# A diagonal recurrence beside latent attention: turning tables made one stage earlier, and four products summed on TensorE

## The chip, the cores and the metric

The kernel runs on one core of a Trainium2 chip. The metric is the device time in microseconds of one launch, the median of several runs. The engines are TensorE (PE in the profile; its weight loads PEld), VectorE (DVE), ScalarE (ACT), GpSimd (POOL) and SyncE (SP), which issues the weight DMAs. They run their own instruction streams and meet at semaphores.

## The reference, cut to what matters

Eight blocks follow each other on 512 positions of 1024 channels: four of a first network, then two layers of a second, each a mixer and a feed-forward block. The change concerns the mixer of the second layer (stage "o") and the feed-forward block ahead of it (stage "f0"). Stage o projects the input once, runs a diagonal state-space recurrence on 256 of the channels and a latent attention of 6 heads on the others, and multiplies both by the output weights:

```
proj = t @ w_in
y_c = s5_ssm(proj[..., :256], ...)            # recurrence
y_d = mla_attention(c_q, c_kv, k_r, ...)      # attention
out = concatenate([y_c, y_d]) @ w_out

# s5_ssm: complex state of 16 groups x 64, mag and angle per state from a_re, a_im, log_dt
x[s] = (mag * exp(i * angle)) * x[s-1] + bu[s]
y = x_re @ c_re - x_im @ c_im + d_skip * u
z = gelu(y);  y_c = z * sigmoid(z @ w_glu + b_glu)
```

## The kernel before, in words

Everything stays in SBUF; activations are kept transposed (128 channels by 512 positions a tile). Each fp32 product is made of three fp32r matmuls (`product`, L286 to L299): high weights by high activations, high by low, low by high. Weights come in units of 128 by 1024 through two raw buffers and four slots. SyncE loads a unit when VectorE has split the one two before it, ScalarE makes its high part (`split_high`, L276), VectorE its low part (`split_low`, L283). The splits are called three units ahead (`AHEAD`).

A feed-forward stage works in three groups of 8, 8 and 6 tiles of gate and up products with a SiLU between them and an output product behind each group; `tail_*` and `head_*` carry one stage into the next by halves of the positions. While a stage's norm is still being summed, its first four units are multiplied unnormed and scaled later by the reciprocal root (`late_keep`, L424).

**Stage o** follows a list written out by hand, `o_events` (L2086), which all engines walk through: "head" (units 0 to 3), "bu" (input products of a state tile), "u" (units 4 and 5), "state n" (VectorE's recurrence up to instruction n), "sum" and "norm" (the norms of the latent tiles), "kn", "v", "uq" (keys, values, queries), "cy" (output products of a state tile), then 27 "step"s: in step n the scores of block n, the softmax of it on VectorE and ScalarE, the transposes of block n-2 and the values of block n-3. Every step takes up to four state instructions with it, until all are done.

**The recurrence** has eight state tiles of 128 states. Turning the state by its angle makes the complex recurrence two real ones, each a scan (`tensor_tensor_scan`). Per tile VectorE issues 14 instructions, all counted on the semaphore `o_ssm` (L2554 to L2592): 0 to 5 turn the products of `bu` (in PSUM banks 2 and 3) back by the table of cosines and sines, 6 and 7 are the scans, 8 to 13 turn the result forward: four multiplications, a subtraction and an addition give the two parts x_re and x_im in `full`. TensorE multiplies these by `o_c` (L2222), two fp32 matmuls of 32 output rows a tile; each stands as two records in the trace.

**The tables** are made on GpSimd inside stage o (`o_gpsimd`, L2688). By doubling, it makes cosines and sines of 32 fine and 16 coarse positions for all eight tiles; for each tile a wide product of both gives the 512 cosines and sines, six operations of 128 by 512 (L2693, L2737). The buffer `o_e` holds two tiles; tile j waits until tile j-2's 14 instructions are done. The small tables wait for stage e's output, and the fine one is copied when stage o's norm is summed.

**The head of stage o**: ScalarE (L2334 to L2346) runs for m = 0 to 2 a weight split and then copies the product out, and for m = 3 it first keeps the norm scale; VectorE (L2602) does three splits, waits for the scale and scales the two tiles of u, which "bu" needs. VectorE also scales c's coefficients after state instruction 8 (`prepare_c`), and turns one rotary tile per "uq" (`rope`), with `o_w` (that is `ssq`) as scratch, as in the state instructions.

Of the kernel before, what the change touches and what calls it, by code (L numbers as in the profile page):

```python
# [31 lines left out]
P = 128  # L32
# [125 lines left out]
def build(nc, stream, x_in, params_in, const_in, tables_in, ssm_in, x_out):  # L158
# [10 lines left out]
    with ctx:  # L169
# [86 lines left out]
        o_c_done, o_small_done = sem("o_c_done"), sem("o_small_done")  # L256
        o_e_done, o_lin, o_squared, o_sums, o_roots = sem("o_e_done"), sem("o_lin"), sem("o_squared"), sem("o_sums"), sem("o_roots")
        o_rstds, o_normed, o_n_high, o_n_low = sem("o_rstds"), sem("o_normed"), sem("o_n_high"), sem("o_n_low")
        o_rot, o_turned, o_cosed, o_roped = sem("o_rot"), sem("o_turned"), sem("o_cosed"), sem("o_roped")
        o_bu, o_ssm, o_cy, o_taken, o_gelu = sem("o_bu"), sem("o_ssm"), sem("o_cy"), sem("o_taken"), sem("o_gelu")  # L260
# [1824 lines left out]
        O_SSM, O_BANKS, O_PER_STEP = 14, 5, 4  # L2085
        O_STEPS = NBLK * MLA_HEADS + 3  # L2086

        def o_events():

            out = [("head", 0), ("bu", 0), ("state", 8), ("u", 4), ("bu", 1), ("state", 14), ("sum", 0),  # L2090
                   ("cy", 0), ("state", 22), ("u", 5), ("bu", 2), ("state", 28), ("cy", 1), ("sum", 1), ("norm", 0),
                   ("state", 36), ("kn", 0), ("v", 0), ("bu", 3), ("uq", 0), ("state", 42), ("uq", 1), ("cy", 2)]
# [40 lines left out]
        o_tmp = work[:, 1536:2048]  # L2133
        o_ea = work[:, 2048:2304].rearrange("p (c j n) -> p c j n", c=2, j=SSM_TILES)
        o_eb = sq[:].rearrange("p (c j n) -> p c j n", c=2, j=SSM_TILES)
# [11 lines left out]
        O_SOFT = 3  # L2147
        O_EVENTS = o_events()
# [28 lines left out]
        def o_tensor(pe, t, first, o, y_base, r, last=False):  # L2177
# [17 lines left out]
            for event, n in O_EVENTS:  # L2195
# [17 lines left out]
                if event == "cy":  # L2213
# [7 lines left out]
                    for c in range(2):  # L2221
                        mm = nc.tensor.matmul(out, o_c[:, c, m], full[:, c], start=c == 0, stop=c == 1,  # L2222
                                              tile_position=(0, 32 * (m % 4)))
# [101 lines left out]
        def o_scalar(act, first, o, y_base, r, last=False):  # L2325
# [7 lines left out]
            for event, n in O_EVENTS:  # L2333
                if event == "head":  # L2334
                    norm_root(act, R_PRE["o"])
                    for m in range(4):
                        u = Unit(first + m)
                        if m == 3:
                            act.wait_ge(table_loaded, 16 * (TABLED.index("o") + 1))
                            late_keep(act, "o", 7, o_r)  # L2340
                        else:
                            split_high(act, u + 1 + AHEAD)
# [3 lines left out]
                        copy((o_us[:, 0], o_us[:, 1], o_lat[:, 0], o_lat[:, 1])[m], m, (units_done, u.count(1)))  # L2346
                if event == "u":
# [59 lines left out]
                if event == "gelu":  # L2407
                    for m in range(2):
                        act.wait_ge(o_taken, m + 1)
                        nc.scalar.activation(o_us[:, m], o_us[:, m], ACT.Gelu_apprx_tanh).then_inc(o_gelu, 1)  # L2410
                    for m in range(2):
                        act.wait_ge(o_gelu, m + 1)
# [100 lines left out]
        def o_vector(dve, first, o, y_base, r, last=False):  # L2513
# [4 lines left out]
            def rope(n, bank, tile):  # L2518

                dve.wait_ge(o_rot, n + 1)  # L2520
                nc.vector.tensor_tensor(o_w[:], bank, table[:, T:2 * T], ALU.mult).then_inc(o_turned, 1)
# [577 lines left out]
```

## Time and profile before

| what | value |
|---|---|
| median of 3 runs (lowest, highest) | 3076.29 us (3073.81, 3078.74) |
| profiled execution, its span | 3078.95 us, 3077.1 us |
| PE busy, share of the span | 2950.9 us, 96% |
| DVE busy | 1753.1 us, 57% |
| ACT busy | 1061.6 us, 35% |
| POOL busy | 200.3 us, 7% |
| chain that ended last | PE 81%, DVE 10%, ACT 3%, issue 3%, POOL 2% |
| mean granted TensorE clock | 0.976 |

Stage f0 runs from about 2035 to 2440 us and stage o's own work from about 2430 to 2720 us of the span. In the tables below a line number is the line of the kernel; "idle" is the time for which the engine did nothing before an instruction, with what ended it. Overlapping instructions of one engine can start before the one ahead has ended, so the distance of two starts is the better price of one.

### The profile page before, as it was taken

To read this page: it belongs to the slowest core of one execution; us is meant where nothing else is said; L and a number is where in the kernel's file an instruction comes from. 1 tells how busy PE (TensorE), PEld (TensorE's weight loads), DVE (VectorE), ACT (ScalarE), POOL (GpSimd) and SP (SyncE) were. 2 spreads that over 40 slices of the span, in tenths; PEclk is the share of its full clock that TensorE was granted. 3 is DMA by queue.
4 is the path that set the end of the run, shared out by engine and by line. 5 is a ranking of instruction groups with operands and counts; after the bars stand their busy time and mean duration, and the time that the engine had idled before them with its cause. 6 is when DMAs were issued, how large, how long until landed. Compare 5 with 4: busy or idle time off the path is not lost.

```text
span 3077.1 us, 38456 instructions
## 1 busy us (share of the span) xinstructions
PE 2950.9 (96%) x14106; PEld 2411.0 (78%) x14106; DVE 1753.1 (57%) x2644; ACT 1061.6 (35%) x1596; POOL 200.3 (7%) x203
## 2 busy tenths in 40 slices
PE   8999999999999999999999999899999778899998
PEld 6888888888888778878888866588888744788887
DVE  5554536764676576653545586564444588464445
ACT  4332323442344332233322424442223423442222
POOL 1000000000000100000000100020000533110001
PEclk9999999999999999999999999899999888999999
DMA  4232232212221223333232321023333210123332
GB/s 144 96 96 94 85 106 73 60 58 83 75 60 57 83 82 98 97 94 102 83 101 90 103 70 41 16 93 108 94 102 96 69 41 7 55 89 96 95 96 89
DMA packets 70399, 252.12 MB, mean 82 GB/s; under 512 B 7808, under 2 KB 9856, under 8 KB 69632
## 3 DMA queue, kind: packets, MB, share of 16 engines
q1 hardware_dynamic: 68112, 241.89, 25.7%
q10 hardware_dynamic: 2160, 8.49, 0.8%
q8 instruction: 86, 1.41, 0.2%
q14 instruction: 41, 0.34, 0.0%
HBM read 248.25 MB, written 2.10 MB: 81 GB/s over the span
## 4 chain that ended last, share of the span: by engine, by line
PE 81%; DVE 10%; ACT 3%; issue 3%; POOL 2%; DMA 0%; DVEq 0%; ACTq 0%; POOLq 0%
PE ps L296 17%; PE ps L298 17%; PE ps L297 17%; PE ps L567 2%; PE ps L568 2%; PE ps L569 2%; DVE w_low L283 2%; ACT w_high L276 2%; PE ps L778 1%; PE ps L779 1%; PE ps L780 1%; PE ps L1788 1%; PE ps L852 1%; PE ps L590 1%; PE ps L838 1%
## 5 line engine op out<-in xcount | busy, mean ns | idle before, releaser
L283 DVE TENSOR_TENSOR w_low<-raw,w_high 128x1024 fp32r<-128x1024 f32 x456 | 562.2, 1238 | 421.0 <-ACT w_high L276 413.7
L296 PE MATMUL ps<-h_high,w_high 128*128 128x512 f32 x1872 | 738.7, 395 | 5.7 <-DVE arena L1463 3.0
L298 PE MATMUL ps<-h_high,w_low 128*128 128x512 f32 x1872 | 730.7, 390 | 0.0
L297 PE MATMUL ps<-h_low,w_high 128*128 128x512 f32 x1872 | 730.5, 390 | 0.0
L276 ACT ACTIVATE w_high<-raw 128x1024 fp32r<-128x1024 f32 x456 | 477.8, 1051 | 454.8 <-PE ps L298 214.2
L296 PEld LDWEIGHTS ps<-h_high,w_high 128*128 128x128 f32 x1872 | 352.9, 189 | 80.7 <-issue 4.6
L298 PEld LDWEIGHTS ps<-h_high,w_low 128*128 128x128 f32 x1872 | 352.4, 188 | 74.2
L297 PEld LDWEIGHTS ps<-h_low,w_high 128*128 128x128 f32 x1872 | 353.0, 189 | 70.1
L296 PE MATMUL ps<-y_high,w_high 128*128 128x512 f32 x640 | 250.3, 391 | 0.6 <-DVE y_low L1923 0.2
L297 PE MATMUL ps<-y_low,w_high 128*128 128x512 f32 x640 | 249.1, 389 | 0.0
L298 PE MATMUL ps<-y_high,w_low 128*128 128x512 f32 x640 | 249.0, 389 | 0.0
L324 POOL TENSOR_TENSOR root<-root,ssq 128x512 f32<-128x512 f32 x24 | 33.0, 1373 | 1691.8 <-ACT ssq L312 1690.4
L296 PEld LDWEIGHTS ps<-y_high,w_high 128*128 128x128 f32 x640 | 120.1, 188 | 27.8 <-DVE y_low L685 2.0
L298 PEld LDWEIGHTS ps<-y_high,w_low 128*128 128x128 f32 x640 | 120.1, 188 | 25.3
L297 PEld LDWEIGHTS ps<-y_low,w_high 128*128 128x128 f32 x640 | 120.2, 188 | 24.7
L567 PE MATMUL ps<-w_high,h_high 128*128 128x512 f32 x256 | 102.1, 399 | 11.5 <-DVE w_low L283 11.5
L568 PE MATMUL ps<-w_low,h_high 128*128 128x512 f32 x256 | 101.4, 396 | 0.0
L569 PE MATMUL ps<-w_high,h_low 128*128 128x512 f32 x256 | 101.1, 395 | 0.0
L1549 ACT ACTIVATE y_high<-full 128x512 f32 (+1 forms) x44 | 27.8, 632 | 192.6 <-DVE full L1579 192.6
L778 PE MATMUL ps<-w_high,h_high 128*128 128x512 f32 x192 | 76.7, 400 | 3.2 <-DVE x L519 2.1
L779 PE MATMUL ps<-w_low,h_high 128*128 128x512 f32 x192 | 76.0, 396 | 0.0
L780 PE MATMUL ps<-w_high,h_low 128*128 128x512 f32 x192 | 75.8, 395 | 0.0
(403 smaller groups left out, 4573.8 us busy)
## 6 DMA issues: line engine op xcount, KB each, us to landing
raw<-stream SPq DMA_DIRECT2D x456, 512.0 KB, 3.6
table<-tables_in ACTq DMA_DIRECT2D x5, 1088.0 KB, 6.6
x<-x_in ACTq DMA_DIRECT2D x8, 256.0 KB, 8.5
x_out<-x SPq DMA_DIRECT2D x16, 128.0 KB, 1.7
const<-const_in SPq DMA_DIRECT2D x1, 673.0 KB, 8.0
work<-ssm_in ACTq DMA_DIRECT2D x1, 512.0 KB, 3.7
params<-params_in ACTq DMA_DIRECT2D x1, 287.0 KB, 6.8
```

Source lines behind the costliest of these rows:

```text
L276: nc.scalar.activation(w_high[:, u.slot], raw[:, u.raw], ACT.Copy).then_inc(weights_high, 1)
L283: nc.vector.tensor_tensor(w_low[:, u.slot], raw[:, u.raw], w_high[:, u.slot].bitcast(F32), ALU.subtract).then_inc(weights_low, 1)
L296: nc.tensor.matmul(bank, wh, high[:, k], start=k == 0, stop=False)
L297: nc.tensor.matmul(bank, wh, low[:, k], start=False, stop=False)
L298: mm = nc.tensor.matmul(bank, wl, high[:, k], start=False, stop=k == tiles - 1)
L324: nc.gpsimd.tensor_tensor(root[:], root[:], (sq, ssq)[m % 2][:], ALU.add).then_inc(norm_gathered, 1)
L567: nc.tensor.matmul(bank, hh, wh, start=k == 0, stop=False)
L568: nc.tensor.matmul(bank, hh, wl, start=False, stop=False)
L569: mm = nc.tensor.matmul(bank, hl, wh, start=False, stop=k == KD - 1)
L778: nc.tensor.matmul(bank, hh, wh, start=k == 0, stop=False)
L779: nc.tensor.matmul(bank, hh, wl, start=False, stop=False)
L780: mm = nc.tensor.matmul(bank, hl, wh, start=False, stop=k == KD - 1)
```

## The change

The tables are made in a function `o_tables` that GpSimd runs at the start of stage f0, once stage e's residual is added. Tiles 0 and 1 are written to `o_e`, where they stay. Tiles 2 to 7 go through a ring of five buffers in a part of the arena that the feed-forward stage doesn't use, and are stored to a DRAM tensor, 512 KB each. In stage o, GpSimd fetches tile j from there into `o_e` when tile j-2's instructions are done. VectorE waits for the fetch instead of for the computation.

A tile takes 12 instructions on VectorE in place of 14. The four products of the forward turn go to four buffers (`full`, `sq`, `o_w`), one with its sign changed, and cy adds them on TensorE: four matmuls with the same `o_c` in place of two. VectorE's scratch is now `o_t` in `work`. The event list has the counts of 12. In the head, the keeping of the norm scale goes ahead of the third weight split on ScalarE, and the scaling of u ahead of it on VectorE; the split of that unit follows behind the head's copies. The semaphore `o_gelu` is merged into `o_z_high`.

```diff
@@ -2082,14 +2083,14 @@
-O_SSM, O_BANKS, O_PER_STEP = 14, 5, 4
+O_SSM, O_BANKS, O_PER_STEP = 12, 5, 4
...
-    out = [("head", 0), ("bu", 0), ("state", 8), ("u", 4), ("bu", 1), ("state", 14), ("sum", 0),
-           ("cy", 0), ("state", 22), ("u", 5), ("bu", 2), ("state", 28), ("cy", 1), ("sum", 1), ("norm", 0),
-           ("state", 36), ("kn", 0), ("v", 0), ("bu", 3), ("uq", 0), ("state", 42), ("uq", 1), ("cy", 2)]
+    out = [("head", 0), ("bu", 0), ("state", 8), ("u", 4), ("bu", 1), ("state", 12), ("sum", 0),
+           ("cy", 0), ("state", 20), ("u", 5), ("bu", 2), ("state", 24), ("cy", 1), ("sum", 1), ("norm", 0),
+           ("state", 32), ("kn", 0), ("v", 0), ("bu", 3), ("uq", 0), ("state", 36), ("uq", 1), ("cy", 2)]
@@ -2130,9 +2131,12 @@
 o_c = work[:, 1024:1536].rearrange("p (c j h) -> p c j h", c=2, j=SSM_TILES)
-o_tmp = work[:, 1536:2048]
+o_tmp = work[:, 0:512]
+o_t = work[:, 1536:2048]
 o_ea = work[:, 2048:2304].rearrange("p (c j n) -> p c j n", c=2, j=SSM_TILES)
-o_eb = sq[:].rearrange("p (c j n) -> p c j n", c=2, j=SSM_TILES)
+o_eb = work[:, 1536:2048].rearrange("p (c j n) -> p c j n", c=2, j=SSM_TILES)
+o_made = view(5120, 5, 2, T)
+o_kept = nc.dram_tensor("o_turns", (SSM_TILES, P, 2 * T), F32, kind="Internal").ap()
@@ -2145,6 +2149,7 @@
 O_SOFT = 3
+O_STORED = 16 * (SSM_TILES - 2)
@@ -2218,8 +2223,8 @@
             out = ps[32 * (m % 4):32 * (m % 4) + 32, 4]
-            for c in range(2):
-                mm = nc.tensor.matmul(out, o_c[:, c, m], full[:, c], start=c == 0, stop=c == 1,
+            for c, product_of in enumerate((full[:, 0], full[:, 1], sq[:], o_w[:])):
+                mm = nc.tensor.matmul(out, o_c[:, c // 2, m], product_of, start=c == 0, stop=c == 3,
@@ -2332,18 +2337,20 @@
         if event == "head":
+            act.wait_ge(o_e_moved, O_STORED)
...
                 u = Unit(first + m)
-                if m == 3:
+                if m < 2:
+                    split_high(act, u + 1 + AHEAD)
+                if m == 2:
...
                     late_keep(act, "o", 7, o_r)
-                else:
-                    split_high(act, u + 1 + AHEAD)
...
                 copy((o_us[:, 0], o_us[:, 1], o_lat[:, 0], o_lat[:, 1])[m], m, (units_done, u.count(1)))
+            split_high(act, Unit(first + 3 + AHEAD))
@@ -2407,9 +2414,9 @@
                 act.wait_ge(o_taken, m + 1)
-                nc.scalar.activation(o_us[:, m], o_us[:, m], ACT.Gelu_apprx_tanh).then_inc(o_gelu, 1)
+                nc.scalar.activation(o_us[:, m], o_us[:, m], ACT.Gelu_apprx_tanh).then_inc(o_z_high, 1)
             for m in range(2):
-                act.wait_ge(o_gelu, m + 1)
+                act.wait_ge(o_z_high, m + 1)
@@ -2518,11 +2525,11 @@
         dve.wait_ge(o_rot, n + 1)
-        nc.vector.tensor_tensor(o_w[:], bank, table[:, T:2 * T], ALU.mult).then_inc(o_turned, 1)
+        nc.vector.tensor_tensor(o_t, bank, table[:, T:2 * T], ALU.mult).then_inc(o_turned, 1)
...
         dve.wait_ge(o_cosed, n + 1)
-        nc.vector.tensor_tensor(tile, tile, o_w[:], ALU.add).then_inc(o_roped, 1)
+        nc.vector.tensor_tensor(tile, tile, o_t, ALU.add).then_inc(o_roped, 1)
@@ -2554,22 +2561,25 @@
             cos, sin = o_e[:, j % 2, 0], o_e[:, j % 2, 1]
-            b_re, b_im, x_re, x_im = ps[:, 2], ps[:, 3], full[:, 0], full[:, 1]
+            b_re, b_im = ps[:, 2], ps[:, 3]
...
                 dve.wait_ge(o_bu, j + 1)
-                dve.wait_ge(o_e_done, 2 * j + 2)
+                if j < 2:
+                    dve.wait_ge(o_e_done, 2 * SSM_TILES)
+                else:
+                    dve.wait_ge(o_e_moved, O_STORED + 16 * (j - 1))
...
             if n == 1:
-                op(j, o_w[:], sin, b_im, ALU.mult, 0)
+                op(j, o_t, sin, b_im, ALU.mult, 0)
             if n == 2:
-                op(j, o_a[:], o_a[:], o_w[:], ALU.add, 2)
+                op(j, o_a[:], o_a[:], o_t, ALU.add, 2)
...
             if n == 4:
-                op(j, o_w[:], sin, b_re, ALU.mult, 3)
+                op(j, o_t, sin, b_re, ALU.mult, 3)
             if n == 5:
-                op(j, o_s[:], o_s[:], o_w[:], ALU.subtract, 5)
+                op(j, o_s[:], o_s[:], o_t, ALU.subtract, 5)
@@ -2578,17 +2588,15 @@
                     dve.wait_ge(o_cy, j)
-                op(j, x_re, cos, o_a[:], ALU.mult, 7)
+                op(j, full[:, 0], cos, o_a[:], ALU.mult, 7)
             if n == 9:
-                op(j, o_w[:], sin, o_s[:], ALU.mult, 8)
+                dve.wait_ge(o_ssm, O_SSM * j + 8)
+                nc.vector.scalar_tensor_tensor(out=full[:, 1], in0=sin, scalar=-1.0, in1=o_s[:], op0=ALU.mult,
+                                               op1=ALU.mult).then_inc(o_ssm, 1)
             if n == 10:
-                op(j, x_re, x_re, o_w[:], ALU.subtract, 10)
+                op(j, sq[:], sin, o_a[:], ALU.mult, 8)
             if n == 11:
-                op(j, x_im, cos, o_s[:], ALU.mult, 8)
-            if n == 12:
-                op(j, o_w[:], sin, o_a[:], ALU.mult, 11)
-            if n == 13:
-                op(j, x_im, x_im, o_w[:], ALU.add, 13)
+                op(j, o_w[:], cos, o_s[:], ALU.mult, 8)
@@ -2600,12 +2608,13 @@
             norm_rstd(dve, R_PRE["o"])
-            for m in range(3):
+            for m in range(2):
...
                 nc.vector.tensor_tensor(o_us[:, m], o_us[:, m], o_r, ALU.mult).then_inc(o_us_scaled, 1)
+            split_low(dve, Unit(first + 3 + AHEAD))
@@ -2685,7 +2694,7 @@
-def o_gpsimd(pool):
+def o_tables(pool):
@@ -2695,10 +2704,8 @@
     pool.wait_ge(o_prepared, 1)
-    if "e" in names:
-        pool.wait_ge(out_free, 8 * (O_NO["e"] + 1) + 2)
-    early = o_e[:, 1].rearrange("p c (j n) -> p c j n", j=SSM_TILES)[:, :, :, 0:EB]
-    for tab, size, power in ((early, EB, 0), (o_ea, EA, 5)):
+    pool.wait_ge(post_added, 2 * KD * (P_NO["e"] + 1))
+    for tab, size, power in ((o_eb, EB, 0), (o_ea, EA, 5)):
@@ -2718,24 +2725,30 @@
             n, power = 2 * n, power + 1
-    pool.wait_ge(norm_summed, SUMMED[R_PRE["o"]] + 2)
-    nc.gpsimd.tensor_copy(o_eb, early).then_inc(o_small_done, 1)
-    pool.wait_ge(o_small_done, done[0] + 1)
-    done[0] += 1
...
         b_cos_, b_sin_ = (o_eb[:, c, j].unsqueeze(1).to_broadcast(shape) for c in range(2))
-        e_cos, e_sin = (o_e[:, j % 2, c].rearrange("p (a b) -> p a b", a=EA) for c in range(2))
+        target = o_e[:, j] if j < 2 else o_made[:, (j - 2) % 5]
+        e_cos, e_sin = (target[:, c].rearrange("p (a b) -> p a b", a=EA) for c in range(2))
         tmp = o_tmp.rearrange("p (a b) -> p a b", a=EA)
-        if j >= 2:
-            pool.wait_ge(o_ssm, O_SSM * (j - 1))
+        if j == 7:
+            pool.wait_ge(o_e_moved, 16 * 5)
...
             pool.wait_ge(o_e_done, 2 * j + (1 if op == ALU.subtract else 2))
+        if j >= 2:
+            pool.dma_start(o_kept[j], target.rearrange("p c t -> p (c t)")).then_inc(o_e_moved, 16)
+
+def o_gpsimd(pool):
+
+    for j in range(2, SSM_TILES):
+        pool.wait_ge(o_e_moved, O_STORED + 16 * (j - 2))
+        pool.wait_ge(o_ssm, O_SSM * (j - 1))
+        pool.dma_start(o_e[:, j % 2].rearrange("p c t -> p (c t)"), o_kept[j]).then_inc(o_e_moved, 16)
@@ -2852,6 +2865,8 @@
             e_gpsimd(pool)
+        if name == "f0":
+            o_tables(pool)
```

## Rows read from the trace of the kernel before

**Rows 1.** Stage f0 by stretch: length, PE, PEld, DVE, ACT, POOL busy, PEclk, DMA, GB/s.

```profile
2200.00:2300.00 100.00, 100.00 (x443) 82.79 (x442) 44.02 (x49) 25.77 (x30) 0.00 (x0) 1.00 0.32 97
```

**Rows 2.** Waits in stage o: total, times, longest.

```profile
PE ps L2222 <- DVE full L2550: 14.8, 5, 7.7
...
PE ps L2210 <- DVE arena L2608: 6.3, 1, 6.3
...
DVE root L2550 <- POOL arena L2737: 14.6, 1, 14.6
```

**Rows 3.** VectorE in order of time, stage o: start, length, instruction.

```profile
2443.39 1.23 DVE L283 TENSOR_TENSOR w_low<-raw,w_high 128x1024 fp32r<-128x1024 f32 x1 [3.46 <-ACT w_high L276]
2444.84 1.30 DVE L2608 TENSOR_TENSOR arena<-arena,table 128x512 f32<-128x512 f32 x2 [0.23 <-ACT table L424]
2460.77 0.69 DVE L2550 TENSOR_TENSOR root<-arena,ps 128x512 f32<-128x512 f32 x1 [14.63 <-POOL arena L2737]
...
2470.42 0.42 DVE L2535 TENSOR_TENSOR ssq<-work,small 128x256 f32<-128x256 f32 x1
...
2472.81 1.22 DVE L283 TENSOR_TENSOR w_low<-raw,w_high 128x1024 fp32r<-128x1024 f32 x1
...
2498.46 0.16 DVE L2624 SCALAR_TENSOR_TENSOR table<-ps,norm_col 128x4 f32<-128x4 f32 x1 [5.63 <-PE ps L2230]
...
2506.81 0.69 DVE L2550 TENSOR_TENSOR root<-arena,ps 128x512 f32<-128x512 f32 x1
...
2513.03 2.36 DVE L283 TENSOR_TENSOR w_low<-raw,w_high 128x1024 fp32r<-128x1024 f32 x2
...
2525.78 0.69 DVE L2550 TENSOR_TENSOR full<-arena,root 128x512 f32<-128x512 f32 x1
...
2529.76 1.23 DVE L283 TENSOR_TENSOR w_low<-raw,w_high 128x1024 fp32r<-128x1024 f32 x1
```

**Rows 4.** Busy time by stretch, stage o.

```profile
2439.90:2446.20 6.30, 0.00 (x1) 0.00 (x1) 2.55 (x4) 3.90 (x7) 5.38 (x14) 0.92 0.57 172
2446.20:2455.20 9.00, 9.00 (x17) 5.29 (x18) 0.00 (x0) 0.53 (x1) 7.21 (x24) 0.50 0.14 52
...
2535.30:2561.80 26.50, 24.28 (x72) 11.80 (x73) 24.49 (x50) 10.05 (x26) 11.07 (x9) 0.81 0.00 0
2574.60:2620.20 45.60, 39.98 (x142) 19.94 (x141) 41.99 (x89) 17.26 (x46) 7.38 (x6) 0.85 0.00 1
2620.20:2631.40 11.20, 11.20 (x51) 6.20 (x52) 4.95 (x20) 6.96 (x18) 0.00 (x0) 1.00 0.00 0
```

**Rows 5.** TensorE in order of time, stage o.

```profile
2477.95 3.62 PE L2222 MATMUL ps<-full,work 128*32 128x512 f32 x4 [7.66 <-DVE full L2550]
...
2487.70 1.98 PE L2210 MATMUL ps<-arena,work 32*128 32x512 f32 x4
...
2496.41 1.95 PE L2230 MATMUL ps<-const,arena 128*128 128x1 f32 x16
...
2530.57 1.90 PE L2222 MATMUL ps<-full,work 128*32 128x512 f32 x4
```

**Rows 6.** ScalarE in order of time, head of stage o.

```profile
2438.57 0.58 ACT L2329 ACTIVATE arena<-ps 128x512 f32<-128x512 f32 x1
2442.30 1.06 ACT L276 ACTIVATE w_high<-raw 128x1024 fp32r<-128x1024 f32 x1 [3.14 <-DMA raw<-stream]
...
2444.21 0.60 ACT L424 ACTIVATE table<-ps 128x512 f32<-128x512 f32 x1
```

**Rows 7.** GpSimd's groups from 1990 to 2720 us: busy, mean ns, idle before.

```profile
L2737 POOL TENSOR_TENSOR arena<-arena,work 128x512 f32<-128x512 f32 x16 | 24.4, 1525 | 1.3
...
L2693 POOL TENSOR_TENSOR work<-work,sq 128x512 f32<-128x512 f32 x16 | 18.1, 1128 | 1.3
```

**Rows 8.** TensorE's waits at the start of stage f0.

```profile
PE ps L296 <- DVE arena L1571: 0.5, 1, 0.5
```

**Rows 9.** DMA issues of the page: count, size, time to landing.

```profile
raw<-stream SPq DMA_DIRECT2D x456, 512.0 KB, 3.6
```

More of the change, by code:

```diff
@@ L256, in build @@
         o_c_done, o_small_done = sem("o_c_done"), sem("o_small_done")
+        o_e_moved = sem("o_e_moved")
         o_e_done, o_lin, o_squared, o_sums, o_roots = sem("o_e_done"), sem("o_lin"), sem("o_squared"), sem("o_sums"), sem("o_roots")
@@ L259, in build @@
         o_rot, o_turned, o_cosed, o_roped = sem("o_rot"), sem("o_turned"), sem("o_cosed"), sem("o_roped")
-        o_bu, o_ssm, o_cy, o_taken, o_gelu = sem("o_bu"), sem("o_ssm"), sem("o_cy"), sem("o_taken"), sem("o_gelu")
+        o_bu, o_ssm, o_cy, o_taken = sem("o_bu"), sem("o_ssm"), sem("o_cy"), sem("o_taken")
         o_z_high, o_z_low, o_sig, o_gated, o_small = sem("o_z_high"), sem("o_z_low"), sem("o_sig"), sem("o_gated"), sem("o_small")
@@ L2649, in o_vector @@
                 if event == "uq":
-                    assert at % O_SSM in (0, 8)
+                    assert at % O_SSM not in (2, 5)
                     rope(n + 1, ps[:, o_turn_bank(n)], o_q[:, n % 2, 2])
@@ L2675, in o_vector @@
                     for m in range(2):
-                        dve.wait_ge(o_z_high, m + 1)
+                        dve.wait_ge(o_z_high, m + 3)
                         nc.vector.tensor_tensor(h_low[:, 3 + m], o_us[:, m], h_high[:, 3 + m].bitcast(F32),
```

## The prediction

> **What bounds the kernel now.** The page comes first: TensorE is busy 96% of the span, so time can only be won where it is not. The busy table by stretch and TensorE's waits then lead to stage o. In the feed-forward stage before it TensorE has no gap in 100 us [rows 1]; in stage o it waits for VectorE: 14.8 us for the state products ahead of the cy matmuls, 6.3 us for the scaled u [rows 2]. VectorE's own waits show what is behind it: it stands 14.6 us for GpSimd's first turning table [rows 2]. The order in time says what surrounds that: VectorE is ready at 2444.84 + 1.30 = 2446.1, its first state product starts at 2460.77, and the argument of the second norm is taken at 2498.46 [rows 3]. From there to the first scores the stage is a mixed chain over all engines; in the softmax steps that follow, TensorE and VectorE are both nearly full, at a granted clock of 0.81 and 0.85 [rows 4].
>
> Two properties matter. While GpSimd builds tables, the first eight state instructions of a tile take 2470.42 - 2460.77 = 9.65 us; with GpSimd silent they take 2513.03 - 2506.81 = 6.2 [rows 3]. The 3.4 us between lie on the two additions and two scans: 0.86 each. And TensorE's clock falls behind idle time: after the 6.3 us gap it is 0.50 for 9 us [rows 4]; four cy records took 3.62 us cold and 1.90 warm [rows 5].
>
> **Head.** ScalarE keeps the norm scale only behind a weight split that waits 3.14 us for its DMA, at 2444.21 [rows 6]. The change puts it ahead of that split. ScalarE is free at 2438.57 + 0.58 = 2439.15 [rows 6]; it keeps the scale until 2439.75, and two squares and two copies, each some 0.48 behind the last, end at 2441.7. VectorE scales u meanwhile (1.30 us, [rows 3]), from 2439.9 to 2441.3. So bu of tile 0 starts at 2441.75 instead of 2446.2, after 1.9 us of idle, in which I expect the clock to stay (0.92 is its mean over all of the 6.3 us gap, [rows 4]). It takes 1.98 warm [rows 5], until 2443.7. Behind the scaling VectorE now has the split of unit 6, whose weights come when they came before: it ends at 2443.39 + 1.2 = 2444.6 [rows 3], and there the state products start, 16.1 us earlier than at 2460.77.
>
> **To the second norm sum, walked forward.** VectorE: eight instructions 6.2 us (2450.85); the coefficients of c, 2472.81 - 2470.42 = 2.4 [rows 3], and a split of 1.2 (2454.45); then the second half of the tile. That was six instructions in 2529.76 - 2525.78 = 4.0 us [rows 3]; it becomes four independent ones at 0.6, 2.45 us. The new scalar_tensor_tensor is priced like the others; at 1 us it would cost 0.4 a tile. Tile 0 is ready at 2456.9. TensorE, warm: unit u4 with 24 matmuls at 0.226 (443 in 100 us, [rows 1]) 5.4 us, bu of tile 1 2.0, the first norm sum 1.0 (half of the second's 1.95, [rows 5]): done at 2452.1, then idle for 4.8. I take the clock as fallen. Cy has four products in place of two, eight records: 7.2 us cold, 3.8 warm; with cold for about 4.5 us and warm from there it is 5.9, until 2462.8. Now TensorE is the later one: u5 5.4, bu 2.0, cy of tile 1 3.8 (VectorE has it ready at 2467.3), second sum 1.95: 2476.0. That point was 2498.46 [rows 3]: 22.5 us won. If the clock takes 9 us to come back, as in [rows 4], it is 20.5; if it never falls, 24.6; at half clock all the way, 11.4.
>
> **Norm to the first scores.** The rope addition loses its contention (0.9 us won, as above). Cy of tile 2 is twice as long, +1.9 on TensorE, of which VectorE's rope, also freed of GpSimd, gives 0.7 back: -1.2. Kn, v, uq and their weights keep their order, and cost what they did.
>
> **Steps.** Steps 1 to 18 carried four state instructions each. 17 of these intervals took 26.5 + 45.6 = 72.1 us [rows 4], 4.24 each; with the 18th, and without the third uq unit among them, 76.3. Four steps without any took 11.2 us, 2.8 each [rows 4]. 96 instructions instead of 112 need steps 1 to 15, and three steps fall to 2.8: 8.4 us. In a step with state VectorE needs (6.2 + 2.45)/3 and 1.2 of softmax (4.95 us busy over four steps, [rows 4]): 4.1. TensorE needs 2.3 for scores, transposes and values (11.2 less a cy of 1.9, over four) and (1.98 + 3.8)/3: 4.2 at full clock, 5.0 at this stretch's 0.84. I take 4.5, between them: 15 x 4.5 + 8.4 = 75.9, only 0.4 won. At 4.2 it is 4.9 won, at 5.0 7.1 lost. One seventh of VectorE's instructions is nearly paid away here by the longer cy.
>
> **Tables in stage f0.** Moved are 16 groups of three wide operations (24.4 us for one of the three, 18.1 for another, [rows 7], the third about the same: some 62 us), the narrow doubling ones, and six new stores of 512 KB issued behind them. GpSimd is otherwise idle in that stage, and its next task, the gathering at the stage's end, is over 200 us away. It meets VectorE's splits, gate products and y_low, which read two SBUF operands. TensorE's lead is small at the stage's start, where it waited 0.5 us for a gate copy [rows 8], but only narrow operations run then. Later a pair of units is 10.8 us on TensorE and 4.8 on VectorE (44.02 us in 100, [rows 1]); four blocked instructions at up to 1 us still fit. I charge 1 us, bounds 0 and 8. Without that cover the price would be some 0.86 us for each blocked instruction. ScalarE's new wait for the stores stands far behind them.
>
> **Fetches.** Tile j is fetched over GpSimd's queue once tile j-2 is finished; one whole tile, at least 3 x 4.1 = 12 us in the steps, lies between that and its use. No DMA of this queue is in the trace. The nearest, 512 KB of weights, land in 3.6 us [rows 9]; I take up to twice that, so nothing, and beyond 12 us five tiles would pay each microsecond. Nothing is queued behind these waits on GpSimd that another engine needs before the stage's end. The page "SBUF — State Buffer" of the Trainium skill ("SBUF: two separate sides") warns that a DMA from GpSimd's queue can be starved of descriptors by some VectorE instructions, 620 ns becoming about 3100. By that page the landing would be 6.1 us, an estimate, still hidden; no row here shows it.
>
> **Sum.** 22.5 + 0.9 - 1.2 + 0.4 - 1.0 = 21.6 us. The profiled execution took 3078.95 (span 3077.1), the median of the runs is 3076.29; 3078.95 - 21.6 = 3057.35, on the scale of the median 3054.7.
>
> **Rivals.** (a) The clock stays up: the head gives 24.6, a step costs 4.2, f0 nothing: 24.6 + 0.9 - 1.2 + 4.9 = 29.2, so 3047.1. For it, cy of tile 2 ran warm within busy work [rows 5]; against it, the clock of 0.81 and 0.85 in the steps. (b) TensorE becomes the bound of the steps at that same clock, 5.0 each: 22.5 + 0.9 - 1.2 - 7.1 - 1.0 = 14.1, so 3062.2. For it, TensorE is nearly full there already; against it, some of its low clock came from waiting. (c) GpSimd's port use in f0 eats the lead: with VectorE's chain at 12.2 us instead of 10.8 over six pairs of units, 8 us, so 3061.7. For it, the 9.65 against 6.2 us; against it, the lead grows to several us first. The same page ("Who interferes with whom") has such an instruction fully blocked behind GpSimd's; by that rule, the trace agrees, 0.86 us each. (d) Slower: the doubled cy keeps TensorE near half clock in the steps. 21.2 us are won ahead of them, so it decides from (76.3 + 21.2 - 8.4)/15 = 5.9 us a step, a mean clock of 0.71. At 0.65 a step is 6.5: 97.5 + 8.4 - 76.3 = 29.6 lost, 3084.7. For it, 0.50 for 9 us after the gap; against it, no long stretch of steps was below 0.81. (e) The table was not the last wait and another, the weights', takes its place at once: within 0.2% of before. Against it: unit 6 was split and ready 16 us before the first product.
>
> **Chances.** Forecast 0.40, (a) 0.16, (b) 0.20, (c) 0.10: faster by over 0.2% 0.86 (0.2%, 6 us, is about what a measurement of this kernel can tell from no change). (e) 0.06. (d) 0.08, with it the small chance of fetches beyond 16 us, which would end there too. The range, 3045 to 3066, takes in (a), (b), (c), and (b) with half of (c); it leaves out (d) and (e).
>
> **What would show it.** The first state product near 2444.6 with no wait for GpSimd; the second norm's argument 22 us earlier; cy with eight records in 3.8 us warm; 15 steps with state at 4.5 us; GpSimd busy some 85 us in f0 with TensorE still gapless; each fetch landed ahead of its tile. A gap of TensorE in f0, or state steps over 5 us, would make the prediction wrong, and so would a wait of VectorE for a fetch.

## The result, and the profile after

The changed kernel takes 3065.8 us (median of 10 runs, 3063.95 to 3071.69) against 3076.28 (10 runs, 3073.05 to 3081.14): ratio 0.9966, 95% interval [0.9957, 0.9976]. 10.5 us are won where 21.6 were forecast. The profiled execution took 3063.99 us, its span is 3062.2, the mean granted clock 0.981.

The page has VectorE 14.3 us less busy and GpSimd 19.3 us more; the two kinds of new DMA land in 3.0 and 3.6 us, like the weights in [rows 9]. From the page (busy time; DMA issues):

```profile
PE 2950.9 (96%) x14138; PEld 2405.5 (79%) x14138; DVE 1738.8 (57%) x2628; ACT 1061.2 (35%) x1596; POOL 219.6 (7%) x214
...
PE 84%; DVE 8%; ACT 3%; issue 3%; DMA 1%; POOL 1%; DVEq 0%; ACTq 0%; POOLq 0%; SPq 0%
...
o_turns<-arena POOLq DMA_DIRECT2D x6, 512.0 KB, 3.0
arena<-o_turns POOLq DMA_DIRECT2D x6, 512.0 KB, 3.6
```

Two profiled executions don't reach stage o at the same time: this one has VectorE's norm reduction of stage o (L396) at 2431.17 us, that of before 2435.80, and those 4.63 us arose before the tables are made in stage f0: the norm reduction of f0 itself is 4.66 us apart (2052.97 and 2057.63), and nothing is changed ahead of it. So places in stage o are compared from that reduction on. VectorE in order of time, the answer to [rows 3]:

```profile
2435.22 1.29 DVE L2616 TENSOR_TENSOR arena<-arena,table 128x512 f32<-128x512 f32 x2
2438.74 1.23 DVE L284 TENSOR_TENSOR w_low<-raw,w_high 128x1024 fp32r<-128x1024 f32 x1 [2.24 <-ACT w_high L277]
2439.89 0.68 DVE L2557 TENSOR_TENSOR root<-arena,ps 128x512 f32<-128x512 f32 x1
...
2446.09 0.42 DVE L2542 TENSOR_TENSOR ssq<-work,small 128x256 f32<-128x256 f32 x1
...
2449.62 0.68 DVE L2557 TENSOR_TENSOR full<-arena,root 128x512 f32<-128x512 f32 x1
2450.22 0.68 DVE L2594 SCALAR_TENSOR_TENSOR full<-arena,rstd 128x512 f32<-128x512 f32 x1
...
2471.57 0.16 DVE L2633 SCALAR_TENSOR_TENSOR table<-ps,norm_col 128x4 f32<-128x4 f32 x1 [9.04 <-PE ps L2235]
```

The wait for GpSimd is gone: the first product (L2557, root) starts 8.72 us after the norm's reduction, where it was 24.97. Eight state instructions take 2446.09 - 2439.89 = 6.2 us and no longer 9.65. The second norm's argument (last row) comes 40.40 us after the reduction, before 62.66: 22.3 us won there. But it waits 9.04 us for TensorE.

The waits of stage o, the answer to [rows 2]:

```profile
DVE ps L2670 <- PE ps L2318: 18.3, 10, 4.8
PE ps L2227 <- DVE ssq L2557: 13.6, 5, 4.5
DVE arena L2681 <- PE ps L2227: 11.0, 2, 5.8
DVE table L2633 <- PE ps L2235: 9.0, 1, 9.0
```

Both engines wait for each other, by turns: TensorE for the four products ahead of cy (second line), VectorE for the scores (first) and for the norm sum behind cy (last). The third line is VectorE's "take", an event that stands in the list directly behind cy 3 and cy 7: one instruction (L2681) that adds the finished sum of four tiles to u. VectorE waits in it for the whole cy and does no state instruction meanwhile. The softmax steps from step 1 to step 23, first of the kernel before, then of the one after (columns of [rows 4]):

```profile
2535.29:2631.40 96.11, 84.99 (x300) 43.47 (x301) 79.62 (x171) 38.78 (x98) 26.47 (x21) 0.88 0.02 6
```

```profile
2508.66:2616.56 107.90, 92.14 (x320) 43.52 (x321) 68.48 (x159) 38.09 (x98) 1.62 (x3) 0.89 0.06 20
```

VectorE is busy 11.1 us less, and the steps take 11.8 us longer: TensorE is busy 7.2 us more (92.14 against 84.99) and idle 4.6 us more. This is where the missing gain went.

### The profile page after: what moved, and what is told of

It reads as the page before. It is cut to its first block, busy times and chain, and to the rows that moved or that the text cites. A ratio compares the mean times of both kernels' runs of the same rounds, so it can differ in the third digit from the quotient of the medians.

```text
span 3062.2 us, 38510 instructions
## 1 busy us (share of the span) xinstructions
PE 2950.9 (96%) x14138; PEld 2405.5 (79%) x14138; DVE 1738.8 (57%) x2628; ACT 1061.2 (35%) x1596; POOL 219.6 (7%) x214
## 4 chain that ended last, share of the span: by engine, by line
PE 84%; DVE 8%; ACT 3%; issue 3%; DMA 1%; POOL 1%; DVEq 0%; ACTq 0%; POOLq 0%; SPq 0%
PE ps L297 17%; PE ps L299 17%; PE ps L298 17%; PE ps L568 2%; PE ps L570 2%; PE ps L569 2%; ACT w_high L277 2%; DVE w_low L284 2%; PE ps L779 1%; PE ps L781 1%; PE ps L780 1%; PE ps L2227 1%; PE ps L1789 1%; PE ps L853 1%; PE ps L591 1%
## 5 line engine op out<-in xcount | busy, mean ns | idle before, releaser
L284 DVE TENSOR_TENSOR w_low<-raw,w_high 128x1024 fp32r<-128x1024 f32 x456 | 569.5, 1254 | 417.0 <-ACT w_high L277 410.0
```

The source lines that it names most:

```text
L284: nc.vector.tensor_tensor(w_low[:, u.slot], raw[:, u.raw], w_high[:, u.slot].bitcast(F32), ALU.subtract).then_inc(weights_low, 1)
```

## The experiments

All times below are medians, each kernel compared with runs of the kernel before on the same chip; the third column counts, in each profile, from VectorE's norm reduction of stage o to the first softmax (the memset ahead of it), the fourth from there to the last one, 23 steps on. `halfcy` and `halfcy_later` leave two of the four products out of cy; their result lacks them.

| kernel | us, ratio to before [95%] | to first step | steps |
|---|---|---|---|
| before | 3076.3 | 98.18 | 97.42 |
| after | 3065.8, 0.9966 [0.9957, 0.9976] | 76.17 | 109.22 |
| oldhead | 3068.8, 0.9978 [0.9969, 0.9987] | 80.67 | 108.17 |
| halfcy | 3050.7, 0.9929 [0.9916, 0.9943] | 71.00 | 101.87 |
| vsums | 3045.9, 0.9907 [0.9892, 0.9922] | 72.44 | 93.44 |
| later | 3053.4, 0.9930 [0.9917, 0.9944] | 76.27 | 95.39 |
| halfcy_later | 3044.9, 0.9907 [0.9891, 0.9922] | 70.89 | 93.83 |
| vsums_later | 3055.5, 0.9938 [0.9923, 0.9952] | 72.23 | 102.24 |
| v_order | 3044.6, 0.9893 [0.9878, 0.9908] | 71.61 | 94.04 |
| v_order_later | 3056.0, 0.9931 [0.9917, 0.9946] | 71.34 | 106.51 |
| v_apart | 3045.0, 0.9898 [0.9878, 0.9917] | 72.39 | 91.72 |
| later_order | 3052.1, 0.9922 [0.9905, 0.9938] | 72.26 | 95.89 |
| halves | 3060.1, 0.9943 [0.9927, 0.9960] | 76.23 | 102.88 |
| v_order_apart | 3047.5, 0.9898 [0.9880, 0.9915] | 71.45 | 96.42 |

**The parts of the change.** First the head alone is put back:

```diff
-                if m < 2:
+                if m < 3:
                     split_high(act, u + 1 + AHEAD)
-                if m == 2:
+                if m == 3:
...
-            split_high(act, Unit(first + 3 + AHEAD))
```

(and VectorE's three splits ahead of the scaling likewise).

> The changed kernel with the old order in the head: ScalarE keeps the norm scale behind the third weight split, VectorE scales u behind it. If the reorder is worth what the forward walk said, bu of tile 0 starts 4.4 us later and finds a fallen clock: 4.4 to 6 us slower, 3070 to 3072. Rival: the start of the state is not on the path, cy of tile 0 and 1 being bound by TensorE's clock: under 1.5 us.

It took 3068.8 us, 3.0 more (0.0012 by ratio, 3.7, the intervals overlap): between the two ranges. In the trace the first state product comes 14.21 us behind the norm's reduction in place of 8.72, the second norm's argument and the first step 4.5 us later, and the steps give 1.05 us back.

Then the sums are put back on VectorE, with tables and head as changed: 14 instructions a tile, two products in cy.

```diff
-O_SSM, O_BANKS, O_PER_STEP = 12, 5, 4
+O_SSM, O_BANKS, O_PER_STEP = 14, 5, 4
...
-        nc.vector.scalar_tensor_tensor(out=full[:, 1], in0=sin, scalar=-1.0, in1=o_s[:], op0=ALU.mult,
-                                       op1=ALU.mult).then_inc(o_ssm, 1)
+        op(j, o_t, sin, o_s[:], ALU.mult, 8)
     if n == 10:
-        op(j, sq[:], sin, o_a[:], ALU.mult, 8)
+        op(j, full[:, 0], full[:, 0], o_t, ALU.subtract, 10)
...
+        op(j, full[:, 1], full[:, 1], o_t, ALU.add, 13)
```

> The tables part of the change alone: tables in stage f0 and the new head, but 14 instructions a tile on VectorE, with subtraction and addition there and two products in cy. Theory A: the head still wins about 20 us, the steps keep their 4.2 us and lose only GpSimd's contention, so 3050 to 3056, faster than the changed kernel by 10 to 16 us. Rival B (VectorE is the bound of the steps and the two instructions are worth having): 3066 or slower. My prediction's own price of the sums (0.4 us won in the steps, 1.9 lost ahead of them) would put it within 3 us of the changed kernel.

3045.9 us: 30 us below before, 20 below the change, and more than theory A had. So the tables and the head alone are worth nearly three times what the whole change brought, and the four products on TensorE cost 0.9966 - 0.9907 = 0.0059, 18 us: 3.7 ahead of the steps (76.17 - 72.44) and 15.8 in them. Against the kernel before, the steps are 4.0 us shorter (97.42 - 93.44); GpSimd is silent there now, and VectorE's busy time for the same instructions falls from 79.62 to 74.87 us.

Next, the products stay in their four buffers and cy uses only two:

```diff
-for c, product_of in enumerate((full[:, 0], full[:, 1], sq[:], o_w[:])):
-    mm = nc.tensor.matmul(out, o_c[:, c // 2, m], product_of, start=c == 0, stop=c == 3,
+for c, product_of in enumerate((full[:, 0], full[:, 1])):
+    mm = nc.tensor.matmul(out, o_c[:, c, m], product_of, start=c == 0, stop=c == 1,
```

> The changed kernel with two products per tile in cy instead of four: the products kept in sq and o_w are left out, so this run computes only half of the turned state; VectorE still issues its 12 instructions a tile. Theory A (the doubled cy is what took the gain back): the two added matmuls cost 1.9 us a tile warm and up to 3.6 cold, on the path from tile 0 on, so 8 tiles give back 12 to 18 us: 3048 to 3054 against 3065.8. Rival B (not cy but the even rhythm of 12 instructions in 3 steps is what costs): at most 3 us are won, 3063 or more.

3050.7 us, as theory A had it. The doubled matmuls cost 0.0037, 11.4 us. But this kernel has less work than vsums on VectorE and the same on TensorE, and its steps take 8.4 us longer. So a second thing costs beside the length of cy.

The counterpart, the sums alone in the kernel before, wasn't tried: there `sq` holds the small table and GpSimd's scratch lies where `o_t` is now, so the four products and their scratch have no room without a new layout.

**Where cy stands.** With 12 instructions a tile and four a step, each cy of the steps stands in the list straight behind the four products it reads. TensorE and VectorE of the changed kernel at tile 3:

```profile
2517.67 0.79 PE L2318 MATMUL ps<-arena 64*128 64x128 f32 x2
2520.22 3.62 PE L2227 MATMUL ps<-full,work 128*32 128x512 f32 x4 [1.76 <-DVE ssq L2557]
2523.64 1.91 PE L2227 MATMUL ps<-sq,work 128*32 128x512 f32 x2
2525.34 1.28 PE L2227 MATMUL ps<-ssq,work 128*32 128x512 f32 x2
```

```profile
2519.48 0.68 DVE L2557 TENSOR_TENSOR ssq<-arena,rstd 128x512 f32<-128x512 f32 x1
...
2526.66 0.75 DVE L2681 SCALAR_TENSOR_TENSOR arena<-arena,params,ps 128x512 f32<-128x512 f32 x1 [5.79 <-PE ps L2227]
...
2530.01 0.11 DVE L2670 MEMSET ps<- 64x64 f32 x1
```

TensorE finishes the scores, waits 1.76 us for VectorE's last product, runs cy from 2520.22 to some 2526.6 at a low clock, and only then makes the next scores. VectorE meanwhile waits 5.79 us for cy in "take". The granted clock (third number from the end) in ten of these microseconds, and in the five around the 3.99 us wait ahead of cy 7:

```profile
2515.00:2525.00 10.00, 8.24 (x19) 3.49 (x18) 5.57 (x13) 2.34 (x6) 0.54 (x1) 0.53 0.17 53
2590.00:2595.00 5.00, 1.98 (x3) 0.54 (x4) 3.49 (x10) 2.34 (x6) 0.00 (x0) 0.57 0.00 0
```

0.53 and 0.57 are close to the lower level, 1.2 of 2.4 GHz. The clock is down before the wait of 1.76 us already: the scores in the first row took 0.79 us, warm ones of that size 0.48. Cy of tile 2, behind busy work, takes 3.6 us (in the same trace 1.90, 1.02 and 1.02 from 2502.73 on). The test puts cy from tile 3 on one step later in the list; the "take" behind cy 3 and cy 7 moves with it:

```diff
+    was = at
     for n in range(O_STEPS):
...
-        if next_cy < SSM_TILES and at >= O_SSM * (next_cy + 1):
+        if next_cy < SSM_TILES and was >= O_SSM * (next_cy + 1):
...
+        was = at
         if n > 0 and at < O_SSM * SSM_TILES:
```

> The changed kernel with each cy from tile 3 on put one step later in the event list, so that TensorE finds the state finished and VectorE has a step of state instructions to do while cy runs. Theory A1 (in the steps TensorE and VectorE wait for each other in turn at cy: TensorE 9 us for the state, VectorE 18 us for the scores behind cy): 6 to 10 us are won, 3056 to 3060. Rival A2 (TensorE's own work with the doubled cy is the bound at the granted clock, wherever cy stands): at most 2 us, 3064 or more.

3053.4 us, 12 less (0.0036 by ratio, 11), with the same instructions, and better than theory A1 had. There the scores of that size are as slow (0.79 us at 2520.54), but cy 3 comes only behind the next scores, without a wait, when the clock is back:

```profile
2525.05 0.77 PE L2320 MATMUL ps<-arena 64*128 64x256 f32 x2
2525.74 1.90 PE L2229 MATMUL ps<-full,work 128*32 128x512 f32 x4
2527.48 1.02 PE L2229 MATMUL ps<-sq,work 128*32 128x512 f32 x2
2528.34 1.02 PE L2229 MATMUL ps<-ssq,work 128*32 128x512 f32 x2
```

All five later cy's start with a first record of 1.90 us. Its steps, whole, at a clock of 0.95 in place of 0.89:

```profile
2511.48:2605.55 94.07, 86.79 (x320) 43.77 (x321) 68.56 (x160) 38.08 (x98) 1.62 (x3) 0.95 0.07 23
```

How much of this is the place of cy, and how much that of "take", wasn't tested by itself. The step times bound it: of the 13.8 us that the steps got shorter (109.22 - 95.39), 6.8 lie in the two steps at cy 3 and the two at cy 7, where a "take" moved too, and 7.0 in the others, where only cy moved. VectorE's waits in "take" fell from 11.0 to 5.0 us.

**Length against place.** The shift with the halved cy completes a square:

> The changed kernel with cy from tile 3 on one step later, and with only two of the four products in cy (those in sq and o_w are left out of the sum, so the result lacks them): TensorE does half of cy's work, VectorE's 12 instructions are the same. It tells what the doubled cy costs once it does not stand directly behind its producer. With four products the same placement took 3053.4, with two products and the old placement 3050.7. Theory (both matter: two products fewer of 1.9 us a tile, cold ones more): 8 tiles at 1 to 1.5 us, 8 to 12 us less than 3053.4, so 3042 to 3045; and 6 to 9 us below 3050.7. Rival (the doubled cy is free once it does not wait): 3052 to 3054. Rival (the shift helps only the long cy): 3050 to 3051.

3044.9 us, at the upper end of the theory's range. In the steps of the traces, doubling costs 7.4 us where cy stands behind its producer (109.22 - 101.87) and 1.6 a step later (95.39 - 93.83); ahead of the steps, where the place is the same, 5.2 and 5.4. The shift is worth 13.8 us with four products and 8.0 with two. So in the steps the price of the doubled cy is mostly that of its place. Over the whole kernel less of it goes: 0.0023 by ratio, 7.1 us, of the 11.4 stay, most of them ahead of the steps. And this kernel, two VectorE instructions a tile short of vsums and with no more work on TensorE, has the same ratio as vsums, 0.9907, and steps of 93.83 us where vsums has 93.44. In these two lists, taking one seventh of the state instructions from VectorE is worth nothing that could be measured, even if the sums were free; the intervals leave room for some 4.5 us either way.

The same shift in the kernel with 14 instructions:

> The 14-instruction kernel with the tables made early and the new head (sums on VectorE, two products in cy), and cy from tile 3 on placed one step later in the event list. Without the shift it took 3045.9 us and TensorE waited 11.6 us for the state products, 5 times. Theory (cy stands directly behind its producer and its price depends on that; with 14 instructions only 3 of the 5 cy's of the steps had no slack): 1 to 4 us less, 3042 to 3045. Rival (what the shift gave the changed kernel, 12.5 us, came from the doubled cy alone, so two products have nothing to win): within 1 us of 3045.9. Second rival (a shift also delays the last tile and the work behind it): 1 to 4 us more.

All three theories missed: 9.6 us slower than vsums. The trace shows bu and cy in one piece, ahead of the next scores, twice in the steps; the second time:

```profile
2563.59 0.70 PE L2320 MATMUL ps<-arena 64*128 64x256 f32 x2
2565.72 1.98 PE L2217 MATMUL ps<-arena,work 32*128 32x512 f32 x4 [1.43 <-DVE work L2559]
2567.63 3.12 PE L2229 MATMUL ps<-full,work 128*32 128x512 f32 x4
...
2572.20 0.81 PE L2319 MATMUL ps<-arena 128*128 128x384 f32 x2
```

14 is no multiple of 4, so the step in which a tile ends shifts, and the later cy falls into the step of the next bu. Bu waits for VectorE, cy runs behind it at a lower clock (3.12 us, not 1.90). VectorE waits for the late cy at its instruction 8 (the first product into `full`), and for the scores:

```profile
2570.79 0.69 DVE L2559 TENSOR_TENSOR full<-arena,root 128x512 f32<-128x512 f32 x1 [1.26 <-PE ps L2229]
...
2574.00 0.11 DVE L2674 MEMSET ps<- 64x64 f32 x1 [1.92 <-PE ps L2320]
```

To test this, bu is put two instructions later, so that it leaves that step:

```diff
-        if next_bu < SSM_TILES and at >= O_SSM * (next_bu - 1) + O_BANKS:
+        if next_bu < SSM_TILES and at >= O_SSM * (next_bu - 1) + O_BANKS + 2:
```

> The 14-instruction kernel with cy one step later took 3055.5 us, 9.6 more than without the shift. In its trace cy then stands directly behind the bu of the next tile in some steps (1.98 + 3.12 us between two steps' scores, and bu itself waits for VectorE), because 14 is no multiple of the four instructions of a step. Here bu goes into the event list two instructions later, so that in such a step it moves behind the next one and the two are apart again. Theory (what costs is how much TensorE work stands between one step's scores and the next): most of the 9.6 us comes back, 3045 to 3049. Rival (what costs is VectorE's eighth instruction waiting for the later cy): stays at 3053 to 3056. Rival (the later bu becomes a wait of its own): above 3056.

3045.0 us, 10.5 back, as the theory had it. The wait at instruction 8 went too, so the two causes are not parted by it; the steps, without and with the edit:

```profile
2506.10:2607.04 100.94, 88.54 (x300) 45.97 (x301) 75.00 (x170) 38.59 (x98) 1.62 (x3) 0.83 0.06 21
```

```profile
2504.80:2595.22 90.42, 79.36 (x300) 40.80 (x301) 74.81 (x171) 38.33 (x98) 1.61 (x3) 0.94 0.07 24
```

The same 300 records of TensorE take 88.54 us at a clock of 0.83, and 79.36 at 0.94: 9.2 of the 10.5 us by which the steps got shorter are busy time of TensorE at the lower clock, 1.3 are idle time.

Splitting the long cy, on the kernel of `later`:

```diff
+        if next_half < SSM_TILES and at >= O_SSM * (next_half + 1):
+            out += [("half", next_half)]
+            next_half += 1
...
+    parts = range(4) if m < 3 else range(2) if event == "half" else range(2, 4)
```

> The same 12-instruction kernel (3053.4 us) with cy of tiles 3 to 7 in two halves: the products of full in the step in which they are ready, the two in sq and o_w one step later. The work of TensorE is the same. Theory (what costs is the lump between two steps' scores; a half of 1.9 us fits better than 3.8): 2 to 5 us less, 3048 to 3051. Rival (a product directly behind its producer costs whatever its length, as TensorE waits for VectorE and VectorE for the scores behind it; that wait returns with the first half): 3 to 8 us more, 3056 to 3061.

3060.1 us, 6.7 more (0.0013 by ratio, 4, and the intervals overlap), in the rival's range; in the traces the steps take 7.5 us longer. The first half of tile 3 waits for its producer again and runs at the lower clock:

```profile
2524.17 3.62 PE L2234 MATMUL ps<-full,work 128*32 128x512 f32 x4 [1.71 <-DVE ssq L2565]
```

```profile
DVE ps L2678 <- PE ps L2326: 21.1, 12, 4.7
PE ps L2234 <- DVE ssq L2565: 9.6, 4, 4.7
```

Those of tiles 4 and 7 are as slow (3.62 and 3.56 us), those of 5 and 6 take 1.9. In the steps a short product behind its producer costs more than a long one a step later (101.87 us for `halfcy` and 102.88 here, 95.39 for `later`). The first half waits here for all 12 instructions of its tile, though the two products it reads are ready two instructions sooner; an earlier start wasn't tried.

**Ahead of the steps.** Here u5 goes ahead of cy 0, and the second sum and the norm ahead of cy 1:

```diff
-   ("cy", 0), ("state", 22), ("u", 5), ("bu", 2), ("state", 28), ("cy", 1), ("sum", 1), ("norm", 0),
-   ("state", 36), ("kn", 0), ("v", 0), ...
+   ("u", 5), ("cy", 0), ("state", 22), ("bu", 2), ("state", 28), ("sum", 1), ("norm", 0),
+   ("state", 36), ("kn", 0), ("cy", 1), ("v", 0), ...
```

> The 14-instruction kernel (3045.9 us) with its events ahead of the steps reordered: unit u5 goes ahead of cy of tile 0, and the second norm sum and the norm go ahead of cy of tile 1, which stands behind kn. Both take TensorE's waits directly behind the state products away: 6.2 us ahead of cy 0 and 3.9 us before the second sum. Theory (TensorE's waits there are on the path to the first scores): the second norm's argument comes 4 to 7 us earlier, 3039 to 3042 in all. Rival (the path is VectorE's there, with the same instructions in the same order): within 1.5 us of 3045.9.

3044.6 us, in the rival's range. The norm's argument comes 3.0 us earlier (2468.57 - 2433.13 against 2470.86 - 2432.44), the first step only 0.8, and the ratios' intervals overlap. On the 12-instruction kernel with cy later:

> The 12-instruction kernel with four products and cy from tile 3 on one step later (3053.4 us) with the events ahead of the steps reordered: u5 ahead of cy 0, the second norm sum and the norm ahead of cy 1, which goes behind kn. The same edit in the 14-instruction kernel brought the norm's argument 3.0 us forward and the first softmax step 0.8. Here VectorE waited 9.0 us for the second sum (3.9 there), so TensorE is the later of the two. Theory: 4 to 6 us of that wait go, 3047 to 3050. Rival (as in the 14-instruction kernel, the two cy's only move into the stretch behind the norm): within 1.5 us of 3053.4.

3052.1 us (six runs, 3043.8 to 3058.3): the time is in the rival's range. The trace, which is of the fastest of them, has the first step 4.0 us earlier (76.27 to 72.26) and the steps 0.5 longer, which favours the theory; the time leaves it open.

The last two combine the edits of the 14-instruction kernel, v_order with the shift, and with the shift and bu apart:

> The reordered 14-instruction kernel with cy from tile 3 on one step later as well. Theory (the two act in different stretches and add): the reordering's gain of 4 to 7 us plus the shift's of 1 to 4, 3036 to 3041. Rival (each hides the other, as the steps are bounded by VectorE once the waits are gone): no more than the better of the two alone, by 0.5 us.

> The 14-instruction kernel with all three edits of the event list: the order ahead of the steps, cy one step later, bu two instructions later. With cy later alone on that order it took 3056.0 us. Theory (bu and cy in one step are the whole price of the shift, on this order too): 9 to 12 us come back, 3044 to 3047, and as the order alone gave 3044.6 and the spread bu and cy alone 3045.0, the two together give at most the 0.8 us of the order's first softmax more. Rival (the price on this order has a second source, the wait of the recurrence for cy at its eighth instruction): only half comes back, 3049 to 3052.

3056.0 us: neither theory, the shift again costs 11 us. With bu apart 3047.5, just beyond the upper end, and by ratio (0.9898) equal to v_apart. Its steps in the trace take 96.42 us against 91.72, at a clock of 0.84, with the same list from the first step on; why the clock was lower there stays open, and the trace is of the slowest of its four runs (3051.1). The four fastest kernels that compute everything all have 14 instructions a tile: vsums, v_order, v_apart and v_order_apart (0.9907, 0.9893, 0.9898, 0.9898). Their intervals overlap; they are 29 to 33 us below before by ratio.

## Why the prediction was wrong

**Head, right.** Measured from the norm's reduction, the first product was due at 2444.6 - 2435.80 = 8.8 us and came at 8.72, with no wait for GpSimd. TensorE's gap ahead of bu was 1.8 us (1.9 forecast), and oldhead prices the reordering at 3 to 3.7 us in time, 4.5 to the first step.

**To the second norm sum, right.** 22.5 us forecast, 22.3 measured. The forecast of a 4.8 us gap and a fallen clock ahead of cy 0 holds line by line:

```profile
2452.16 3.62 PE L2227 MATMUL ps<-full,work 128*32 128x512 f32 x4 [4.50 <-DVE ssq L2557]
2455.57 1.91 PE L2227 MATMUL ps<-sq,work 128*32 128x512 f32 x2
2457.28 1.18 PE L2227 MATMUL ps<-ssq,work 128*32 128x512 f32 x2
...
2465.96 1.90 PE L2227 MATMUL ps<-full,work 128*32 128x512 f32 x4
```

Cy 0 took 6.3 us (5.9 forecast), cy 1 3.6 (3.8 forecast). The scalar_tensor_tensor took 0.68 us, as priced. **Norm to the first scores, right:** 0.3 us lost forecast, 36.83 and 37.09 us measured from the norm's argument to step 1.

**Tables in stage f0, covered.** I charged 1 us, and the traces show none: from the norm reduction of f0 to that of stage o it is 378.20 us, before 378.17. TensorE has the same 0.5 us wait at the start as in [rows 8], and no new one of over 0.5 us, while GpSimd is busy 27.93 of 30 us:

```profile
2100.00:2130.00 30.00, 30.00 (x134) 24.86 (x133) 20.11 (x19) 8.97 (x11) 27.93 (x21) 1.00 0.43 140
```

**Fetches, right.** No wait of VectorE for one is in the trace. They landed in 3.6 us in the midst of VectorE's products. The starved queue of which the Trainium skill warns ("SBUF — State Buffer", "SBUF: two separate sides"), an estimate of 6.1 us by that page, wasn't seen here.

**Steps, wrong.** The step of the prediction that failed is "I take 4.5, between them: 15 x 4.5 + 8.4 = 75.9, only 0.4 won". The 14 intervals with state and without the uq unit took 31.82 + 38.79 = 70.6 us, 5.04 each, which is rival (b)'s 5.0 and beyond what the prediction allowed itself ("state steps over 5 us"); the step of cy 7 took 8.3 where I had 2.8 (2593.04 to 2601.31), since that cy stands behind the last state instruction, waits 3.99 us for it and starts at half clock. In all 11.8 us were lost. The sum with that in place of 0.4 won is 22.3 - 0.3 - 11.8 = 10.2 us, and 10.5 were measured. (The two profiled executions are 14.96 us apart, 10.3 without the 4.63 from before stage f0.)

The error has two parts. I averaged a step over three, as if TensorE's work could be spread. It is a chain: scores, then cy, then the next scores, and what cy waits for is VectorE's last instruction of that step; behind cy 3 and cy 7 VectorE also stands still in "take". At the clock of 0.89 that the steps had, TensorE's 4.2 us a step would be 4.7, an estimate; the rest of the 5.04, and the 5.5 us more at cy 7, are not in a mean of work. And I took the clock from the kernel before, 0.84, for a level of that stretch, and wrote for (d) only of a clock kept down by the work of cy. It moves with the order of the list: the same instructions ran at 0.89 and 0.95 (after, later), and at 0.83 and 0.94 (vsums_later, v_apart). With 14 instructions a tile, two of the five cy's of the steps had two instructions of slack, since 14 is no multiple of 4. With 12 none has any. In the steps TensorE of vsums waited 4.8 us for the products (3 times), that of halfcy 10.4 (4 times).

Of the rivals, (b) had the size and part of the cause: its 7.1 us are close to TensorE's 7.2 us of more busy time (in part by luck, as it reckoned with a clock of 0.84), but the 4.6 us of more idle time it didn't have, nor that most of both goes with one step of shift: `later` has 5.4 us less of busy and 8.5 less of idle time than the change. Rival (a), the clock stays up, comes nearest in `later`, whose steps run at 0.95: 2.0 us are won in them where (a) had 4.9, and 22.9 in all of its 29.2.

**What I didn't ask:** what the sums' share was. The prediction found that "One seventh of VectorE's instructions is nearly paid away here by the longer cy"; the square shows no worth of it that could be measured, even with the short cy.

## What to carry to other kernels

Where two engines alternate in short steps, price an edit by the place of each piece of work in the order list: between which two results it stands and what it waits for there; a mean per step hides it. Changing a count (14 to 12 instructions, four a step) changes where everything falls, so re-lay the list with it, and try a product one step behind its producer, apart from other long pieces: in the list of 12 that won 11 us, in the list of 14 it cost 10 beside bu and nothing that could be measured apart from it. Here VectorE waited for TensorE within the steps, so taking work off VectorE and adding some to TensorE lost time: undo such a part alone before it is kept.

## What the runs showed of the hardware

- The granted clock followed the order of events: behind waits of 1.8 to 4.5 us a cy of 3.6 us took 5.3 to 6.4, and behind one of 1.5 us it stayed at 3.6 (cy 5, below). Moving one event moved the mean of 90 to 100 us of steps between 0.83 and 0.94. Which wait of several lowers it isn't resolved by these traces; at tile 3 it was low before the wait.

```profile
2561.89 1.90 PE L2227 MATMUL ps<-full,work 128*32 128x512 f32 x4 [1.46 <-DVE ssq L2557]
```

- With GpSimd at work on the tables, scans are slowed as well as additions of two SBUF tiles. Addition and first scan of tile 0, before and after:

```profile
2464.69 1.57 DVE L2550 TENSOR_TENSOR rstd<-rstd,ssq 128x512 f32<-128x512 f32 x1
2466.18 2.06 DVE L2574 TENSOR_TENSOR_SCAN root<-small,root 128x512 f32<-128x512 f32 x1
```

```profile
2443.12 0.69 DVE L2557 TENSOR_TENSOR rstd<-rstd,work 128x512 f32<-128x512 f32 x1
2443.73 1.22 DVE L2584 TENSOR_TENSOR_SCAN root<-small,root 128x512 f32<-128x512 f32 x1
```

- A 512 KB DMA from GpSimd's queue cost GpSimd 0.54 to 0.58 us to issue in stage o (0.60 to 0.73 in stage f0), and landed as fast as one from SyncE's (fetches 3.6 us, weights 3.6).
